# Earlier adaLN conditions, no stored copy of layer 0's input, and MLA attention issued in pairs of heads

## The reference

```python
for l in range(DEPTH):
    shift, scale, gate = split(silu(cond) @ ada_w[l] + ada_b[l])   # cond is c_ctx or c
    h = rms_norm(x, norm_pre[l]) * (1 + scale) + shift
    o = mixer[l % 3](h)
    x = x + gate * rms_norm(o, norm_post[l])
# MLA: keys and values of a head come from a 512-wide compressed ckv of 512 keys
k, v = split((ckv @ w_ukv).reshape(b, t, 16, 256), [128])
p = softmax((q_nope @ k.T + q_rope @ k_rope.T) * scale)            # 128 + 64 wide
out = ((p @ v).reshape(b, t, 2048) * silu(gate)) @ w_out
```

## Time and profile before

| | us |
|---|---|
| Median of 3 runs (lowest, highest) | 3410.16 (3408.97, 3417.31) |
| The profiled execution, its own time | 3413.34 |
| Span of the profiled execution | 3411.6 |
| PE busy | 3181.1 (93% of the span) |
| DVE busy | 1464.5 (43%) |
| ACT busy | 1063.3 (31%) |
| POOL busy | 203.7 (6%) |
| First attention stage, layer 0 | from 697.8 to 921.2 |
| Second attention stage, layer 3 | from 3038.5 to 3260.0 |

### The profile page before, as it was taken

The page is one execution under the profiler, slowest core; times in us unless marked ns, Lnnn a source line. Parts: engine busy times, 40 slices in busy tenths (PEclk is TensorE's granted clock), DMA queues, the critical chain, the costliest instruction groups (busy, mean ns, idle before and its releaser), DMA issues.

```text
span 3411.6 us, 47297 instructions
## 1 busy us (share of the span) xinstructions
PE 3181.1 (93%) x20134; PEld 2659.9 (78%) x20134; DVE 1464.5 (43%) x2146; ACT 1063.3 (31%) x1441; POOL 203.7 (6%) x321
## 2 busy tenths in 40 slices
PE   5699999989899999989999899999999999999988
PEld 2488788866677888878877777887787998986777
DVE  3499862334434222643244354223344323344443
ACT  1333333232324222223233243223324223322322
POOL 1033330000000110000000000000000000000000
PEclk8799899999999999999999999999999999999999
DMA  9899886521254798795542565555443444321132
GB/s 357 320 314 350 310 315 214 198 75 43 78 207 167 234 258 290 254 368 179 206 167 102 179 212 183 187 206 189 172 149 121 132 128 131 115 87 38 38 129 94
DMA packets 290545, 639.19 MB, mean 187 GB/s; under 512 B 22048, under 2 KB 55472, under 8 KB 280864
## 3 DMA queue, kind: packets, MB, share of 16 engines
q1 hardware_dynamic: 264048, 524.58, 44.7%
q0 software_dynamic: 26288, 111.59, 9.3%
HBM read 561.01 MB, written 75.04 MB: 186 GB/s over the span
## 4 chain that ended last, share of the span: by engine, by line
PE 70%; PEld 7%; DMA 7%; DVE 5%; issue 4%; ACT 3%; PEldq 2%; DVEq 1%; ACTq 0%; POOL 0%; SPq 0%; POOLq 0%
PE bank L302 35%; PE bank L306 21%; PE bank L331 5%; DMA raw<-in_ada_w 3%; PEld bank L770 3%; PEld bank L764 2%; DMA raw<-in_s_w_in 1%; DVE w_lo L406 1%; PE bank L2365 1%; DVE arena L1996 1%; DMA raw<-in_mla_w_in 1%; PEld bank L820 1%; PE bank L346 1%; PE bank L609 1%; ACT hT_hi L456 1%
## 5 line engine op out<-in xcount | busy, mean ns | idle before, releaser
L406 DVE TENSOR_TENSOR w_lo<-raw,w_hi 128x2048 fp32r<-128x2048 f32 (+3 forms) x364 | 619.1, 1717 | 1183.7 <-ACTq L400 1180.4
L302 PE MATMUL bank<-hT_hi,w_hi 128*128 128x384 f32 (+1 forms) x2608 | 903.5, 346 | 34.1 <-DVEq L407 16.0
L399 ACT ACTIVATE w_hi<-raw 128x2048 fp32r<-128x2048 f32 (+3 forms) x364 | 521.6, 1452 | 1301.0 <-PE bank L302 578.6
L302 PE MATMUL bank<-hT_lo,w_hi 128*128 128x384 f32 (+1 forms) x2608 | 887.3, 340 | 0.0
L302 PE MATMUL bank<-hT_hi,w_lo 128*128 128x384 f32 (+1 forms) x2608 | 886.4, 340 | 0.0
L302 PEld LDWEIGHTS bank<-hT_hi,w_hi 128*128 128x128 f32 (+1 forms) x2608 | 493.3, 189 | 99.6 <-issue 71.0
L302 PEld LDWEIGHTS bank<-hT_lo,w_hi 128*128 128x128 f32 (+1 forms) x2608 | 493.2, 189 | 1.6 <-issue 0.6
L302 PEld LDWEIGHTS bank<-hT_hi,w_lo 128*128 128x128 f32 (+1 forms) x2608 | 493.0, 189 | 1.5 <-issue 0.6
L306 PE MATMUL bank<-w_hi,hT_hi 128*128 128x512 f32 x1056 | 424.7, 402 | 12.5 <-DVE hT_lo L460 12.2
L306 PE MATMUL bank<-w_hi,hT_lo 128*128 128x512 f32 x1056 | 419.6, 397 | 0.0
L306 PE MATMUL bank<-w_lo,hT_hi 128*128 128x512 f32 x1056 | 419.5, 397 | 0.0
(11 more groups left out here) (325 smaller groups left out, 2764.1 us busy)
## 6 DMA issues: line engine op xcount, KB each, us to landing
raw<-in_ada_w SPq DMA_DIRECT2D x192, 1024.0 KB, 5.4
raw<-in_mla_w_in SPq DMA_DIRECT2D x64, 768.0 KB, 7.1
raw<-in_gla_w_in SPq DMA_DIRECT2D x48, 1024.0 KB, 7.5
raw<-in_mla_w_in SPq DMA_DIRECT2D x40, 1024.0 KB, 6.9
raw<-in_mla_w_out SPq DMA_DIRECT2D x32, 1024.0 KB, 5.1
raw<-in_s_w_in SPq DMA_DIRECT2D x32, 1024.0 KB, 9.9
s_out_dram<-arena POOLq DMA_DIRECT2D x32, 512.0 KB, 6.0
s_in_dram<-arena POOLq DMA_DIRECT2D x16, 1024.0 KB, 9.0
```

What stands on the lines that cost most here:

```text
L302: mm = nc.tensor.matmul(banks[m][0:width, 0:TOK], wp[:, slot, k, at:at + width], hp[:, kt, :], start=(first and n == 0), stop=(last and n ...
L399: nc.scalar.activation(dst, src_, ACT.Copy)
L406: nc.vector.tensor_tensor(dst, src_, pick(w_hi, *part)[0], ALU.subtract)
```

## The change

The conditions, then the identity, come first among POOL's transfers and have a semaphore of their own (`conditions_in`); PE turns only 32 rows of them, and ACT, which has loaded its SiLU table already, takes the SiLU from PSUM. The other vectors are turned behind adaLN group 0. In layer 0, x is not stored; it is fetched from the inputs, and those who waited for the store wait for the last turn of x on PE (`x_free`). The drains of PE in attention, behind the adaLN turns and behind the S5 state go; the last matmul of the step raises the semaphore. In attention the scores of a pair are computed together: per tile of tokens both 128-wide products, then both rotary products with 64 rows each, the one head's in rows 0 to 63 and the other's in rows 64 to 127, so no padded keys are needed. The order on PE, ACT and DVE is by pairs, and ACT and DVE change places in copying pieces.

```diff
@@ -343,8 +346,8 @@
-        nc.tensor.matmul(banks[5][:, at:at + 2], ada_rows(a)[:, j * P:(j + 1) * P], ada_pick, start=True, stop=True)
-    nc.tensor.drain().then_inc(ada_turned, 1)
+        mm = nc.tensor.matmul(banks[5][:, at:at + 2], ada_rows(a)[:, j * P:(j + 1) * P], ada_pick, start=True, stop=True)
+    mm.then_inc(ada_turned, 1)
...
+def x_free(eng, l):
+
+    if parked(l) == 1:
+        eng.wait_ge(norm_turned, KT)
+    else:
+        eng.wait_ge(x_saved, 16 * (parked(l) - 1))
 
-        nc.scalar.wait_ge(x_saved, 16 * (1 + a // 28))
+        x_free(nc.scalar, a // 28)
@@ -547,13 +558,18 @@
-    pe.wait_ge(inputs_in, 16 * INPUT_LOADS)
-    for a in range(4):
-        mm = nc.tensor.transpose(banks[0][:, a * P:(a + 1) * P], rows_v[:, a, :], ident[:, :])
-    mm.then_inc(rows_turned, 1)
-    pe.wait_ge(silu_ready, 1)
+    pe.wait_ge(conditions_in, 16 * 3)
+    nc.tensor.transpose(banks[6][:, 0:32], rows_v[0:32, 0, :], ident[0:32, 0:32]).then_inc(rows_turned, 1)
+    pe.wait_ge(silu_ready, 2)
     for a in range(ADA_START):
         pe_ada(pe, a)
+        if a == 0:
+            pe.wait_ge(inputs_in, 16 * INPUT_LOADS)
+            for n in range(4):
+                mm = nc.tensor.transpose(banks[7][:, n * P:(n + 1) * P], rows_v[:, n, :], ident[:, :])
+            mm.then_inc(rows_turned, 1)
+        if a == 2:
+            pe.wait_ge(vecs_ready, 1)
         pe_s5_fills(pe, a)
@@ -737,7 +753,7 @@
-    if j % 2 != (eng == "dve"):
+    if j % 2 != (eng == "act"):
...
-            if j == 3:
-                mm.then_inc(chunk_used, 1)
-        nc.tensor.drain().then_inc(kv_ready, 1)
-
-    def scores(h):
-
-        pe.wait_ge(kv_copied, 2 * base + 4 * (h // 2) + 2)
-        if h >= 2:
-            pe.wait_ge(exps_ready, base + h - 1)
+        mm.then_inc(kv_ready, 1)
+
+    def scores(pair):
+
+        pe.wait_ge(kv_copied, 2 * base + 4 * pair + 2)
+        if pair:
+            pe.wait_ge(exps_ready, base + 2 * pair)
         for t in range(3):
             a, b = seen(t)
-            out = score_bank(h, t)
-            nc.tensor.matmul(out, qn[:, h, t * P:(t + 1) * P], kT[:, (h // 2) % 2, h % 2, a:b],
-                             start=True, stop=False)
-            nc.tensor.matmul(out, qr[:, h // 2, t * P:(t + 1) * P], kr_pad[:, h % 2, a:b],
-                             start=False, stop=True)
-        nc.tensor.drain().then_inc(scores_ready, 1)
-
...
+            at = slice(t * P, (t + 1) * P)
+            for hh in range(2):
+                nc.tensor.matmul(score_bank(hh, t), qn[:, 2 * pair + hh, at], kT[:, pair % 2, hh, a:b],
+                                 start=True, stop=False, skip_group_check=True)
+            for hh in range(2):
+                rows = slice(hh * ROPE, (hh + 1) * ROPE)
+                mm = nc.tensor.matmul(score_bank(hh, t), qr[rows, pair, at], kr_both[rows, a:b],
+                                      start=False, stop=True, skip_group_check=True)
+        mm.then_inc(scores_ready, 1)
+    def turn_probs(h):
+        pe.wait_ge(probs_ready, base + h + 1)
+        p = p_sb[:, h % 2]
...
-        nc.tensor.transpose(banks[5][:, LAT:LAT + P], p[:, 0, 0:P], ident[:, :])
-        nc.tensor.drain().then_inc(probsT_ready, 1)
-        if pair + 1 < 8:
-            piece(pair + 1, 2 * hh + 1)
+        nc.tensor.transpose(banks[5][:, LAT:LAT + P], p[:, 0, 0:P], ident[:, :]).then_inc(probsT_ready, 1)
+
+    def weighted_sum(h):
+        n, pair, hh = base + h, h // 2, h % 2
...
         for kk in range(3):
-            nc.tensor.matmul(banks[6][:, CTX:TOK], v_[:, 1 + kk, :], pT[:, 1 + kk, :],
-                             start=(kk == 0), stop=(kk == 2))
-        nc.tensor.drain().then_inc(heads_ready, 1)
+            mm = nc.tensor.matmul(banks[6][:, CTX:TOK], v_[:, 1 + kk, :], pT[:, 1 + kk, :],
+                                  start=(kk == 0), stop=(kk == 2))
+        mm.then_inc(heads_ready, 1)
+    for j in range(4):
+    for pair in range(8):
+        more = pair + 1 < 8
+        if more:
+            piece(pair + 1, 0)
+        if pair:
+            weighted_sum(2 * pair - 1)
+        if more:
+            piece(pair + 1, 1)
+        turn_probs(2 * pair)
+        if more:
+            piece(pair + 1, 2)
+        weighted_sum(2 * pair)
+        turn_probs(2 * pair + 1)
+        if more:
+            piece(pair + 1, 3)
+            scores(pair + 1)
+    weighted_sum(HEADS - 1)
...
     st = Stages(nc.scalar)
-    act.wait_ge(inputs_in, 16 * INPUT_LOADS)
+    act.wait_ge(rows_zero, 1)
+    nc.scalar.activation(small[96:128, 62:63], rows_v[96:128, 1, 0:1], ACT.Silu)
+    act.wait_ge(rows_turned, 1)
+    for c in range(2):
+        silu = nc.scalar.activation(silu_c[:, :, c], banks[6][:, c * 16:c * 16 + 16], ACT.Silu)
+    silu.then_inc(silu_ready, 1)
     act.wait_ge(vecs_ready, 1)
-    for c in range(2):
-        silu = nc.scalar.activation(silu_c[:, :, c], vecs[:, 0, c * 16:c * 16 + 16], ACT.Silu)
-    silu.then_inc(silu_ready, 1)
...
+    def probsT_copy(h):
         act.wait_ge(probsT_ready, base + h + 1)
         act_copy(pT[:, 1:3, :], banks[4][:, :].rearrange("p (a b) -> p a b", a=2))
         nc.scalar.drain().then_inc(probsT_copied, 1)
+    for pair in range(8):
+        exps(2 * pair)
+        exps(2 * pair + 1)
+        if pair + 1 < 8:
+            copy_piece("act", l, pair + 1, 1)
+        probsT_copy(2 * pair)
+        if pair + 1 < 8:
+            split_pair("act", l, pair + 2)
+        probsT_copy(2 * pair + 1)
+        if pair + 1 < 8:
+            copy_piece("act", l, pair + 1, 3)
...
-    dve.wait_ge(inputs_in, 16 * INPUT_LOADS)
-    dve.wait_ge(rows_turned, 1)
-    nc.vector.tensor_copy(vecs[:, :, :], banks[0][:, :].rearrange("p (a b) -> p a b", a=4)).then_inc(vecs_ready, 1)
+    dve.wait_ge(rows_turned, 2)
+    nc.vector.tensor_copy(vecs[:, :, :], banks[7][:, :].rearrange("p (a b) -> p a b", a=4)).then_inc(vecs_ready, 1)
...
-    nc.vector.memset(kr_pad, 0.0)
-    nc.vector.drain()
-    for hh in range(2):
-        rows = slice(hh * ROPE, (hh + 1) * ROPE)
-        nc.vector.tensor_copy(kr_pad[rows, hh, :], krT[rows, :])
+    nc.vector.tensor_copy(kr_both, krT)
...
+    def probsT_copy(h):
         dve.wait_ge(probsT_ready, base + h + 1)
         nc.vector.tensor_copy(pT[:, 3, :], banks[5][:, 0:LAT])
         nc.vector.tensor_copy(pT[:, 0, 0:P], banks[5][:, LAT:LAT + P])
         nc.vector.drain().then_inc(probsT_copied, 1)
+    for pair in range(8):
+        maxes(2 * pair)
+        maxes(2 * pair + 1)
+        if pair + 1 < 8:
+            copy_piece("dve", l, pair + 1, 0)
+        normalize(2 * pair)
+        if pair:
+            gate_head(2 * pair - 1)
+        normalize(2 * pair + 1)
+        probsT_copy(2 * pair)
+        if pair + 1 < 8:
+            split_pair("dve", l, pair + 2)
+            copy_piece("dve", l, pair + 1, 2)
+        gate_head(2 * pair)
+        probsT_copy(2 * pair + 1)
@@ -1649,13 +1688,17 @@
         pool.wait_ge(x_added, NT * (parked(l) - 1))
-    nc.gpsimd.dma_start(x_dram.rearrange("t p d -> p t d"), x).then_inc(x_saved, 16)
-    pool.wait_ge(x_saved, 16 * parked(l))
+        nc.gpsimd.dma_start(x_dram.rearrange("t p d -> p t d"), x).then_inc(x_saved, 16)
+        pool.wait_ge(x_saved, 16 * (parked(l) - 1))
     pool.wait_ge(h_lo_ready, h_quarter(f"mix{l}", 3))
-    nc.gpsimd.dma_start(x, x_dram.rearrange("t p d -> p t d")).then_inc(x_back, 16)
+    if l == layers[0]:
+        nc.gpsimd.dma_start(x[:, 0, :], x_prompt).then_inc(x_back, 16)
+        nc.gpsimd.dma_start(x[:, 1:3, :], x_sample).then_inc(x_back, 16)
+    else:
+        nc.gpsimd.dma_start(x, x_dram.rearrange("t p d -> p t d")).then_inc(x_back, 16)
...
-    xp = w["x_prompt"].rearrange("b t d -> (b t) d")
-    xs = w["x_sample"].rearrange("b (a t) d -> (b t) a d", t=P)
-    nc.gpsimd.dma_start(ident[:, :], consts["ident"]).then_inc(inputs_in, 16)
-
     nc.gpsimd.memset(rows_v, 0.0).then_inc(rows_zero, 1)
     pool.wait_ge(rows_zero, 1)
     for name, src in (("c_ctx", w["c_ctx"].rearrange("(k p) -> k p", p=P)),
                       ("c", w["c"].rearrange("b (k p) -> (b k) p", p=P)),
+                      ("ident", None),
-        tile_, col = VEC[name]
-        nc.gpsimd.dma_start(rows_v[col:col + src.shape[0], tile_, :], src).then_inc(inputs_in, 16)
+        if name == "ident":
+            nc.gpsimd.dma_start(ident[:, :], consts["ident"]).then_inc(conditions_in, 16)
+        else:
+            tile_, col = VEC[name]
+            nc.gpsimd.dma_start(rows_v[col:col + src.shape[0], tile_, :], src)\
+                .then_inc(conditions_in if name[0] == "c" else inputs_in, 16)
```

More of the change, by code:

```diff
@@ L244, in chunk_summed @@
             name, g, s = dense[n]
-            if s == 3 and banks_used(name):
+            if not banks_used(name):
+                eng.wait_ge(kv_ready, 4 * sum(not banks_used(k[0]) for k in dense[:n + 1]))
+            elif s == 3:
                 eng.wait_ge(sums_ready, SUMS[name, g] + banks_used(name))
             else:
```

(27 more changed lines are left out.)

82 lines of the change are left out of this document (32 added, 50 removed).

## The result

The kernel after takes 3357.12 us (median of 4 runs, 3353.10 to 3363.72), the kernel before beside it 3410.47 (4 runs): a ratio of 0.984, 95% interval 0.982 to 0.986, some 53 us. The prediction was 3355, range 3338 to 3384. The profiled execution after has a span of 3351.3 us, 60.3 less than before, and is the fastest of its four; the prediction's sum for profiled executions was 55.5. So the total was met. Its terms were not all met, and the experiments show which of the parts paid. One of the four executions of experiment 5 took 8691.79 us, which nothing here explains; the median given there is of all four, the ratio of the other three.

A forecast was written before the change was run, and what follows sets the result against it. PE's matmuls were taken to bound the kernel. Attention 52, adaLN drains 3 and opening 0.5 us summed to 55.5 off the profiled 3413.3, giving 3357.8; the median lies 3.2 lower, so 3355, range 3338 to 3384.

The forecast's parts named there:

- Drains in attention: PE's steps in attention: ten drains per pair go, and all of their 3.9 us per pair is saved.
- New waits: PE before pieces 2 and 3 in the pairwise order: waits for copies add 1.4 us per pair, bounds 0 and 3.9.
- Rotary products: Attention scores: two heads' 64-row products side by side save 1.52 us per pair, less 0.84 for height changes: net 0.68.
- I take 0.14: Attention scores: each change between full and half height costs 0.14 us, from a range of 0.14 to 0.21, six per pair.
- Period 22.8: Attention: one pair takes 22.8 us instead of 25.9, saving 3.1; seven such periods save 22 per stage.
- Stage ends: Attention stage's opening and last pair: some ten drains are lost there, saving 3.9 us per stage.
- adaLN turns: Drains behind adaLN turns outside the opening: 32 of forty count at 0.1 us each, saving 3; bounds 0 and 16.
- I give the drain 0.1 of it: Behind an adaLN turn, 0.15 us are drain and change of form together; the drain is given 0.1.
- Opening and x of layer 0: Kernel's start: full DMA engines leave 0.5 us gain, bounds -1 and 6; layer 0's dropped, hidden store of x gains 0.
- the signs named ahead: Stages about 197 us; no PE waits naming probabilities, no low clock inside a stage, layer 0's first product moving at most 2.
- rival: Ramp opened 3349 (0.12); height drain 3379 (0.08); rotary not parallel 3379 (0.08); restarts stay 3390 (0.07); slower 3528 (0.03); nearly nothing 3405 (0.04).
- my 4.7: Attention softmax: from the scores' end to the end of DVE's division some 4.7 us, covered by 7.2 of PE work.

The follow-up runs named there:

- experiment 5: Kernel after with a pair's scores reordered to two height changes, not six, and one open sum per bank: 3352.80 us, ratio to before 0.9806.
- experiment 2: Kernel before with only PE's drains in attention removed, old order and padded keys kept: 3379.34 us, ratio to before 0.9909.
- experiment 1: Kernel after with the nine drains of a pair in attention put back: 3399.44 us, ratio to before 0.9956.
- experiment 6: Kernel after with DVE's copy of piece 2 put ahead of its split of the next weights: 3344.13 us, ratio to before 0.9787.
- experiment 3: Kernel after with rotary keys padded to 128 rows again: 3366.38 us, ratio to before 0.9867.
- experiments 4: Kernel after with all six 128-wide score products of a pair first, rotary ones behind, which changes what is computed: 3349.60 us, ratio to before 0.9815.
- the ten: The ten profiled kernels without drains behind adaLN turns: between the attention stages 2077.4 to 2085.4 us, mean 2081.1, with the lower clock's cost taken off.
- the repeat: Kernel after, unchanged, run again on one chip beside two other versions: 3361.34 us, ratio to before 0.9850.
- number 11: Kernel after with the drains behind the adaLN turns put back: 3373.30 us, ratio to before 0.9875.

## Why the prediction was right, and where it was not

- **Drains in attention, 3.9 per pair, all of it: right as a price of the drains, shown from both sides.** A pair had ten in the old order; in the new one it has nine steps. Taken out of the old order they give 2.8 per pair after the waits that open (experiment 2), put into the new one they cost 2.3 (experiment 1). The difference to 3.9 is not a cheaper drain: a drain lies beside the wait that would be there without it.
- **New waits, 1.4: measured 1.1.** Before piece 3 0.9, as said, and for the reason said (experiment 6 removes it by moving the copy alone). Before piece 2 0.2 where I said 0.55: ACT's copy of piece 1 (770.00 to 770.60) ended with the transposes. The waits are not due to the order by pairs, though: experiment 2 has as much in the old one (its period of 23.1 is 1.05 above the work of 22.05). I had booked them to the wrong part.
- **Rotary products, net 0.68: measured 0.43** (scores 5.63 for 6.06; 0.33 of the period and 5.8 us of the two stages by experiment 3). Side by side was right. The step that failed is "I take 0.14": the upper bound of my own rows, 0.21, was the right one, and experiments 4 and 5 measure 0.2, half of it on either side of the change.
- **Period 22.8: measured 22.64.** The two errors, 0.25 and 0.3, cancel; that is luck.
- **Stage ends, 3.9 per stage: measured 0.6 and 0.1.** This is the step that failed most. Outside the seven periods a stage had 42.0 and 40.4 us before, and 41.4 and 40.3 after. "The opening of the stage and the last pair lose some ten drains" counted drains that stood beside waits: the four first pieces wait for each other's copies, and the last pair waits for its softmax and copies with or without drains. From a stage's start to its first scores there were 17.27 and 16.22 us before and 17.07 and 16.18 after, and with the drains put back (experiment 1) the stages grew by 14.8 and 16.0, where seven periods alone make 15.8. The stages lost 46.5, not 52.
- **adaLN turns, 3 us: too small.** 0.15 rather than 0.1 each, 4.2 for the 27 turns between the stages and 6 for all forty. "I give the drain 0.1 of it" failed: all of the 0.15 was the drain: without it eight records and the change of form take 0.88 together, the time that I gave to the records alone. The corrected stretches differ by 6.5; the other 2.3 don't lie at the turns and are within the spread of the ten.
- **Opening and x of layer 0, 0.5 and 0: right in size, the reason in part.** Full DMA engines take back PE's earlier start: the turns of x start at 137.2 against 137.4, whether PE starts at 9 or at 17. I had the last chunk and the store of the slices end the opening. The turns wait for neither the store's landing nor, in the repeat, for that chunk (used at 114.96, turns at 135.4), but for the later of two weight loads that are under way beside the store: the last adaLN chunk or layer 0's first weights. That the store is what makes them late is likely but not shown, as no run moved it. I gave PE's first matmul as 11 us; it came at 9, which changes nothing.
- **The 60.3 of the first two profiles** are 46.5 + 6 for the turns + 4 for 7 us less at the lower clock between the stages + 4 that stay within the scatter. So the closeness of the sum (55.5) is in part luck: it had some 7 us too much at the stage ends and 3 too little for the turns, and the profile of after happened to be quick between the stages. The median of all runs of after lies 48 to 53 below before.

Of the signs named ahead, the stages were to be about 197 (200 and 199), no wait was to name the probabilities (none does), and the low clock was to stay out of the stages: it stays out of the seven periods, but shows at a stage's start and end, as before (in the first stage at 694.0 to 700.9 and 881.8 to 888.6). Layer 0's first product moved by 1.2 us (154.2 to 153.0), under the 2 allowed. No rival came true. The softmax chain is 5.3 us long from the scores' end (785.25 to the end of the first division, 790.56), more than my 4.7, and is covered by 7.2.

## What to carry to other kernels

Raise the semaphore from the last matmul of a step; a drain between steps costs up to 0.4 us each, but count only those that don't stand beside a wait that stays. Before reordering a whole pipeline, take its drains out alone: here that gave 39.7 of the 46.5 us won in attention, and the new order nothing measurable by itself. Then look for what the now tight engine waits for: one copy moved ahead of a longer instruction on its engine, one order with two changes of height instead of six, and two pieces of work kept for the last softmax gave 38 us more, where the change itself gave 48 to 53.

## What the runs showed of the hardware

- A change between matmuls of 128 rows and of 64 costs 0.2 us with fp32 operands, 0.1 at the last record ahead and 0.1 at the first behind, whether the block between is two steps or six (periods of 22.64 with six changes, 21.87 with two). Inside the block two 64-row products run side by side at the pitch of one (0.32 for 384 columns).
- At the same place PE's clock falls in one execution and not in another: 54.6 to 74.8 us at the lower level between the stages in thirteen profiles, which alone moves a time by up to 10 us. The lengths of the attention stages repeat to 1 us in after, its repeat and number 11, where the interval of a time is 5 us or more on either side.
